# Bias rows in free partitions, a third stack buffer, a residual turned back by TensorE, and products that nobody reads

## The reference, cut to what matters

```python
for l in range(DEPTH):                                      # DEPTH = 2, ALPHA = sqrt(2)
    sh1, sc1, g1, sh2, sc2, g2 = split(silu(c) @ w_ada[l] + b_ada[l])     # c is one vector
    h = x * (1 + sc1) + sh1
    y = conformer_conv(h, ...) if l == 0 else fox_attention(...) @ w_o
    x = layer_norm(ALPHA * x + (1 + g1) * y, ln_mix_g[l], ln_mix_b[l])
    h = x * (1 + sc2) + sh2
    y = grouped_moe(h, router_w, router_b, w_gate[l], w_up[l], w_down[l])
    x = layer_norm(ALPHA * x + (1 + g2) * y, ln_ffn_g[l], ln_ffn_b[l])
# conformer_conv: u = a * sigmoid(b) of h @ w_pw1; y = 31-tap causal convolution per channel + b_dw;
#                 silu(layer_norm(y)) @ w_pw2 + b_pw2
# shared_kv (layer 1): silu(c) @ w_ada_kv + b_ada_kv shifts and scales x; k, v, forget gates from it
# grouped_moe: every token goes to two experts of one group, (silu(h @ w_gate) * (h @ w_up)) @ w_down
```

## Time and profile before

| | us |
|---|---|
| median of 3 runs | 1353.41 |
| lowest, highest | 1352.75, 1355.64 |
| the profiled execution, its time | 1354.2 |
| its span | 1352.2 |
| PE, DVE, ACT, POOL busy | 1087.2, 447.4, 168.2, 24.9 |
| HBM read | 492.19 MB, 365 GB/s over the span |

### The profile page before, as it was taken

One profiled execution on the slowest core, in us unless ns is written; L12 is line 12 of the kernel. 1 busy time (PEld: TensorE's weight loads), 2 busy tenths in 40 slices (PEclk: granted clock), 3 DMA queues, 4 the chain that ended last, 5 costly groups with the idle time before them and its releaser, 6 DMA issues.

```text
span 1352.2 us, 30588 instructions
## 1 busy us (share of the span) xinstructions
PE 1087.2 (80%) x12942; PEld 637.4 (47%) x12942; DVE 447.4 (33%) x1389; ACT 168.2 (12%) x401; POOL 24.9 (2%) x58
## 2 busy tenths in 40 slices
PE   3898978667999669766899979696699996796665
PEld 1784434334555235422475864353356663453333
DVE  0498145211333113211454340651133231231114
ACT  1103121000111001000210431210010110000001
POOL 1103000000000000000000000000000000000000
PEclk7899969978999689978999999698899998998888
DMA  9975579999999999999997531889999899999990
GB/s 360 385 288 194 234 314 427 425 425 426 425 424 424 426 426 425 424 425 423 418 418 310 248 125 64 371 363 423 425 427 425 340 411 425 425 425 423 425 412 35
DMA packets 56957, 494.70 MB, mean 366 GB/s; under 512 B 4196, under 2 KB 12420, under 8 KB 17176
## 3 DMA queue, kind: packets, MB, share of 16 engines
q1 hardware_dynamic: 55920, 490.75, 87.5%
q10 hardware_dynamic: 744, 2.35, 0.5%
q0 software_dynamic: 192, 0.15, 0.1%
HBM read 492.19 MB, written 1.05 MB: 365 GB/s over the span
## 4 chain that ended last, share of the span: by engine, by line
PE 52%; DMA 36%; DVE 7%; ACT 2%; issue 1%; POOL 1%; ACTq 1%; SPq 0%; DVEq 0%; POOLq 0%
PE PS L1041 22%; DMA ring<-in_w_up_dram 21%; DMA ring<-in_w_gate_dram 8%; PE PS L948 6%; PE PS L1155 4%; DMA ring<-in_w_down_dram 3%; PE PS L1069 3%; DMA work<-in_w_gate_dram 2%; PE PS L1020 2%; PE PS L1279 2%; PE PS L966 2%; PE PS L853 2%; DVE xs L1410 1%; DMA work<-in_conv_ln_b_dram 1%; PE PS L1032 1%
## 5 line engine op out<-in xcount | busy, mean ns | idle before, releaser
L1041 PE MATMUL PS<-ring,work 128*32 128x256 f32 x8160 | 522.5, 412 | 165.7 <-DMA ring<-in_w_up_dram 67.3
L1041 PEld LDWEIGHTS PS<-ring,work 128*32 128x32 f32 x8160 | 282.3, 117 | 391.5 <-issue 116.7
L1593 DVE TENSOR_TENSOR work<-work,PS 128x256 f32<-128x256 f32 x47 | 19.8, 422 | 435.8 <-PE PS L1041 434.5
L948 PE MATMUL PS<-ring,work 128*128 128x512 f32 x192 | 83.3, 594 | 0.5 <-ACT work L804 0.5
L674 ACT ACTIVATE work<-PS 128x256 f32<-128x256 f32 x47 | 18.1, 384 | 436.1 <-PE PS L1041 436.1
L1041 PE MATMUL PS<-work 128*32 128x256 f32 x864 | 56.4, 404 | 15.1 <-DMA work<-in_w_gate_dram 9.7
L1679 DVE SCALAR_TENSOR_TENSOR work<-work,colv 128x256 f32<-128x256 f32 x150 | 67.0, 503 | 1.2
L1020 PE MATMUL PS<-hs,work 128*32 128x256 f32 x784 | 55.6, 402 | 8.8 <-DVE work L1561 7.8
L1155 PE MATMUL PS<-work,ring 128*128 128x256 f32 x256 | 58.3, 392 | 2.5 <-ACT work L615 2.5
L1069 PE MATMUL PS<-work 32*128 32x256 f32 x784 | 56.1, 400 | 3.8 <-DVE work L1606 3.8
L853 PE MATMUL PS<-ring,cact 128*32 128x512 f32 x384 | 49.3, 664 | 11.2 <-DMA ring<-in_w_ada_dram 11.2
(11 more groups left out here) (239 smaller groups left out, 845.5 us busy)
## 6 DMA issues: line engine op xcount, KB each, us to landing
ring<-in_w_gate_dram SPq DMA_DIRECT2D x58, 2048.0 KB, 34.9
ring<-in_w_up_dram SPq DMA_DIRECT2D x58, 2048.0 KB, 34.8
ring<-in_w_down_dram SPq DMA_DIRECT2D x58, 2048.0 KB, 28.6
ring<-in_w_ada_dram SPq DMA_DIRECT2D x24, 2048.0 KB, 20.4
work<-in_w_up_dram SPq DMA_DIRECT2D x6, 2048.0 KB, 19.7
work<-in_w_gate_dram SPq DMA_DIRECT2D x6, 2048.0 KB, 34.7
work<-in_w_down_dram SPq DMA_DIRECT2D x6, 2048.0 KB, 42.7
ring<-in_w_pw_dram SPq DMA_DIRECT2D x8, 1024.0 KB, 12.1
```

The lines of the kernel that those rows point to most:

```text
L948: last = pe.matmul(PS[:, banks + 2 * t + q, :], rows[:, k, t * P:(t + 1) * P], quarter(index + h, kk, KH)[:, q * BANK:(q + 1) * BANK], sta ...
L1041: last = pe.matmul(dst[SLOTS * s:SLOTS * (s + 1), :], rows[:, cc, SLOTS * q:SLOTS * (q + 1)], quarter(load + h, kk, KH)[:, QUART * s:QUART ...
```

## The change

- **Rows.** `rows` gets rows 8 to 43 for the biases and 72 to 87 for the norms, as they lie in memory, by 7 transfers instead of 20, and a row 96 of ones. The ones and biases are no longer added by DVE (`plus` is gone): `bias_rows` does four matmuls (8 records) at the third load of each adaLN group, with a column of `ident` or of `row_or_one`, which picks the bias row alone or with the row of ones. In front of its first matmul it waits for the DVE addition of the group before.
- **Start.** The turning of `colrows` moves from ahead of load 1 to ahead of load 3. `columns` takes one group there, and the norms' columns (`lncol`, `rescol` with ALPHA) are turned after channel part 3.
- **Third stack** in `colrows`, without the wait for the first.
- **b_pw2** is put into the banks first, between mean and variance.
- **Norm.** ACT takes `copy_cols` and `keep_g2` behind its root and its half; ACT normalises 512 columns of token tile 1, DVE the other 512 and tile 0.
- **Residual.** `keep_x` behind the mixing norm and L689 are gone. ACT makes ALPHA*x, turned, from banks 0 to 3 in eight steps of 128x256 into `rT` (the memory of `xs`), and 32 matmuls (64 partitions, 64 columns each, by halves of the array) turn it back into banks 0 to 3.
- **`unread(n)`**: n matmuls 128x256 of constants, whose result is not read: 8 ahead of turning `hs` in both layers, 6 behind the residual of layer 1, 8 ahead of `sum_x` in both.
- The KV columns' addition moves behind `take_xT`; three of the KV loads come ahead of `sel_ready`.

```diff
 def ada_load(index, j, bank):
+    if j == 2:
+        bias_rows(index, bank)
     arrived(index + j)
...
+def bias_rows(index, bank):
+    pe.wait_ge(rows_in, ROWS)
+    pe.wait_ge(ada_added, adas[0])
...
+    for q in range(4):
...
+        last = pe.matmul(PS[32 * q:32 * q + 32, bank, :], from_row, rows[:, :], start=(index == L_ADA1_G0),
+                         stop=False, tile_position=(0, 32 * q), skip_group_check=True)
...
+def unread(products):
+    for _ in range(products):
+        pe.matmul(PS[:, B_Y, 0:SEQ], ident[:, :], cmask2[:, :, :].rearrange("p b n -> p (b n)"), start=True,
+                  stop=True, skip_group_check=True)
...
 # TensorE, moe(l), behind the logits
-                spread_ln(0, l, 0)
-                spread_ln(1, l, 2)
+                def residual():
+                    pe.wait_ge(rT_ready, l + 1)
+                    for t in range(TT):
+                        for k in range(KD):
+                            for half in range(2):
...
+                                pe.matmul(PS[:, bank, at:at + QUART - 3:KH], rT[of, k, t * P:(t + 1) * P], ident[of, of],
+                                          start=(t == 0 and k % KH == 0), stop=True, tile_position=(64 * half, 0),
+                                          skip_group_check=True)
                 if l == 0:
-                    for j in range(ADA_G // 2):
+                    for j in range(ADA_G - 1):
                         ada_load(L_ADAKV, j, B_GATE)
+                else:
+                    residual()
+                    unread(6)
                 pe.wait_ge(sel_ready, l + 1)
...
                 if l == 0:
-                    for j in range(ADA_G // 2, ADA_G):
-                        ada_load(L_ADAKV, j, B_GATE)
-                if l == 0:
-                    pe.wait_ge(ada_added, 4)
+                    ada_load(L_ADAKV, ADA_G - 1, B_GATE)
+                    residual()
+                unread(8)
...
 # ScalarE, moe(l), behind the exponential
+                for k in range(KD):
+                    last = act.activation(rT[:, k, :], PS[:, k // 2, (k % 2) * SEQ:(k % 2 + 1) * SEQ], ACT.Identity,
+                                          bias=rescol[:, 2 + l, k:k + 1], scale=rescol[:, l, k:k + 1])
+                last.then_inc(rT_ready, 1)
...
-                act.wait_ge(spread_used, (3, 8)[l])
-                for b in range(4):
-                    act.activation(PS[:, b, :].rearrange("p (t n) -> p t n", t=TT), xs[:, :, b * QUART:(b + 1) * QUART],
-                                   ACT.Copy, scale=ALPHA).then_inc(sums_begun, 1)
...
 # TensorE, layer 0: from the projection to the turn
-            project(L_PW2, 0, chunk_ready=z_ready)
...
+            project(L_PW2, 0, y_ready, chunk_ready=z_ready, begun=True)
             pe.wait_ge(ada_added, 2)
             spread_mod(0, 2, 4)
             ada(L_ADA0_G2, 6)
             pe.wait_ge(ada_added, 3)
             spread_g2(0)
-            columns(7, 1, 3)
+            columns(7, 2, 4)
+            unread(8)
             turn_n(1)
             moe(L_MOE0, 0)
```

More of the change, by code:

```diff
@@ L581, in _, with load_rows @@
         def _(act):
[L582 to L584 removed]
+            def load_rows(row, src):
+                act.dma_start(rows[row:row + src.shape[0], :], src).then_inc(rows_in, 16)
             for t in range(TT):
@@ L876, in spread_row @@
                 for i in range(2):
-                    q, r = row(i)
-                    last = pe.matmul(PS[:, bank + i, :], pick(q, r, P), rows[32 * q:32 * q + 32, :], start=True, stop=True,
-                                     tile_position=(32 * q, 0), skip_group_check=True)
+                    strip = slice(row(i) // 32 * 32, row(i) // 32 * 32 + 32)
+                    last = pe.matmul(PS[:, bank + i, :], ident[strip, row(i):row(i) + 1].to_broadcast([32, P]), rows[strip, :],
+                                     start=True, stop=True, tile_position=(strip.start, 0), skip_group_check=True)
                     if i == 0:
@@ L934, in h_there, with project @@
                 pe.wait_ge(hT_copied, 4 * hs_turned[0])
-            def project(index, banks, done=None, chunk_ready=None, rows=hT, between=None):
+            def project(index, banks, done, chunk_ready=None, moving=hT, between=None, begun=False):
                 for h in range(2):
@@ L1127, in _ @@
             turn_h(lambda t, k: by_chunk(xs[:, t, :])[:, k // KH, k % KH, :])
[L1128 to L1133 removed]
+            for j in range(1, ADA_G):
+                if j == ADA_G - 1:
+                    pe.wait_ge(colrows_in, COLROWS)
+                    for k in range(KD):
+                        last = pe.transpose(PS[:, 6, k * 40:k * 40 + NROWS], colrows[0:NROWS, k * P:(k + 1) * P],
+                                            ident[0:NROWS, 0:NROWS])
+                    last.then_inc(cols_turned, 1)
                 ada_load(L_ADA0_G0, j, 4)
             pe.wait_ge(ada_added, 1)
[L1136 removed]
+            columns(5, 1, 2)
             h_there()
@@ L1147, in _ @@
                     last.then_inc(taps_spread, 1)
+                if f == 3:
+                    for j in range(4):
+                        last = pe.matmul(PS[:, 5, 16 * j:16 * (j + 1)], rows[:, j:BANK:4], ident[:, NORM_ROW:NORM_ROW + 16],
+                                         start=True, stop=True, skip_group_check=True)
+                        if j == 0:
+                            behind(last)
+                    last.then_inc(lncol_done, 1)
                 if f >= 4:
@@ L1207, in _ @@
             last.then_inc(mean_done, 1)
+            pe.wait_ge(brow_in, 16 * 4)
+            for t in range(TT):
+                for q in range(2):
+                    r = 32 * (2 * t + q)
+                    pe.matmul(PS[:, 2 * t + q, :], ones[r:r + 1, :], brow[r:r + 1, q * BANK:(q + 1) * BANK],
+                              start=True, stop=False, skip_group_check=True)
             for k in range(KD):
@@ L1214, in _ @@
                 ada_load(L_ADA0_G1, j, 4)
-            pe.wait_ge(brow_in, 16 * 4)
-            project(L_PW2, 0, chunk_ready=z_ready)
-            for t in range(TT):
-                for q in range(2):
-                    r = 32 * (2 * t + q)
-                    last = pe.matmul(PS[:, 2 * t + q, :], ones[r:r + 1, :], brow[r:r + 1, q * BANK:(q + 1) * BANK],
-                                     start=False, stop=True)
-            last.then_inc(y_ready, 1)
+            project(L_PW2, 0, y_ready, chunk_ready=z_ready, begun=True)
             pe.wait_ge(ada_added, 2)
@@ L1359, in _ @@
             pe.wait_ge(ada_added, 7)
-            columns(7, 4, 6)
+            columns(7, 5, 7)
+            unread(8)
             turn_n(3)
```

180 lines of the change are left out of this document (92 added, 88 removed).

## The result

| | median, us | ratio to the kernel before |
|---|---|---|
| before | 1353.76 (16 runs) | |
| changed | 1360.17 (16 runs, 1354.91 to 1368.85) | 1.0046 (1.0034 to 1.0059) |

The forecast was 8.1 us faster; the kernel is about 6 us slower. A fence shows the first profile where nothing else is said.

A forecast was written before the change was run, and what follows sets the result against it. Bound: the stream of loads plus its halts when no ring slot is free. Sum: -6.0 - 1.6 + 0.9 - 8.2 + 0.9 + 5.9 = -8.1 us, 1353.4 to 1345.3; range 1339.5 to 1351.5.

The forecast's parts named there:

- Start: Up to the convolution: colrows sooner, loads 1 and 2 done ahead, load 3 ends at 30.5 for 36.4; gain 6.0 us.
- The 3.8 us for thirteen transfers: At the start: thirteen transfers of 0.29 us of issue each go, so colrows come 3.8 us sooner, near 24.
- Convolution's end: Before the mean: without the third stack's 7.86 us, TensorE comes early and waits for VectorE; gain 1.6 us.
- the worst case of POOL's products: In the convolution: POOL's four products beside VectorE's earlier taps may cost 1.4 us at worst; 0 was taken.
- bias_rows: In each adaLN group: eight records of 0.11 us cost 0.9 us, counted where they lie on the path.
- Pause of layer 0: Behind layer 0's projection: first KV load at 22.0 us, slot freed sooner, 8.2 of 8.5 us of standing gained.
- the lid: Layer 0's pause: five loads keep the stream busy until 26.6 us behind the projection, so releases by 25.1 gain the same.
- the cover: Layer 0's pause: three freed loads last to 41.6, gathering at 38.5, so work ahead is free; up to 3 us otherwise.
- Between the layers: From layer 0's experts to the second projection's end: +0.9 us, for bias_rows between two halves of the V projection.
- Pause of layer 1: Behind layer 1's projection: residual (5.8 us) and six products (2.8) precede the count; release at 45.4 for 39.5, loss 5.9.
- rival C: Layer 1's pause: the residual's halves don't overlap, 9.3 us and not 5.8; -4.6 in all, 1348.8 us; chance 0.21.
- Rival D: Both pauses: unread products don't keep the clock, only take time; layer 1 loses 22.9, total +16.4, 1369.8 us; chance 0.09.

The follow-up runs named there:

- e8: The changed kernel with 13 small transfers of 8 numbers each put back ahead of colrows on ScalarE's queue: 1361.99 us, 1.0056 of the kernel before.
- e2: The changed kernel without any unread products, the function and its four calls removed: 1350.50 us, 0.9982 of the kernel before.
- e3: The changed kernel with the norms' rows in four groups of 32 partitions, two read by the spreads here: 1355.44 us, 1.0009 of the kernel before.
- again: The changed kernel measured and profiled once more with no edit: 1359.69 us, 1.0047 of the kernel before.
- e6: Changed kernel, norm rows in four groups, residual behind first expert's gate/up products, unread products only in layer 1 (ten behind logits, seven behind count): 1342.43 us, 0.9909.

## Why the prediction was wrong

**Start: right in kind, -5.5 for -6.0 at best, and -4.6 in the mean.** Load 3 came at 29.3 and not 27, and its sixteen records took 1.92 us, not the 3.5 that I took. The two errors cancel in the first profile (and 36.4 less my 30.5 is 5.9, not 6.0). In the others load 3 took up to 3.64 us, and L1209 starts between 36.7 and 38.6. The 3.8 us for thirteen transfers were not what paid (e8).

**Convolution's end: the step failed.** I said that TensorE would come to the mean early and wait for VectorE. It is TensorE's own queue that comes last: VectorE ends at 120.0, the mean at 121.4. And the change puts the norms' columns, which were in the group of 48 columns ahead of L1155, as eight records of their own between the projections at 60.75, 1.7 us on that queue; I left them out. The 1.4 us that I called the worst case of POOL's products is what VectorE pays at its earlier taps (10.72 for 9.29), and 0.9 of it comes back at the last ones; I had taken 0. It doesn't show, because VectorE is not what comes last. Gain 0.7 for 1.6.

**bias_rows: right.** 1.04 us a group where it is on the path, 0.9 taken.

**Pause of layer 0: the lid was right, the cover wrong.** A gain with nothing behind it is there: 7.3 us in e2, 4.7 to 5.6 in four more profiles, for the 8.2 that I took. In the changed kernel it is 4.1 in the first profile and 2.2 in the mean. Three terms: the eight products ahead of the turn took 5.39 us instead of 3.6, since the clock fell to 0.50 while they ran; the KV loads behind them ran at half clock (6.31 for two); and so the gathering stood at 43.3, behind the 41.6 that I had worked out as its limit and from which I had called all that stands ahead of it free. "It costs up to 3 us if that cover is gone" is what happened. A further 1 us was overlooked. Before, the projection's last product itself frees its slot. In the changed kernel that product signals `y_ready`, the slot is freed with the first product of the spread behind it, and SP's first issue behind the projection (its end at 163.61 before, 158.24 after) moved from 0.04 to 1.09 us behind it. SP's queue, before and after:

```profile
163.65 4.13 SPq L447 DMA_DIRECT2D ring<-in_w_gate_dram  x2
```

```profile
159.33 2.22 SPq L452 DMA_DIRECT2D ring<-in_w_gate_dram  x2
```

With it the first profile closes: 8.3 less 3.2 us of standing less 1.05 is about 4, for 4.1. The 2 us by which the mean gains less lie in the experts behind the pause, or in the chance of before's one profile; no trace here says which.

**Between the layers: a term was missing.** +4.9 for +0.9. `bias_rows` in `sum_acc` is the 0.9. The sum has no term for the two spreads of the norm between the halves of the K projection: I didn't ask on which partitions their rows now lie. Before, the four products read four different groups of 32 rows and ran side by side in 1.14 us; now all read one group and take 3.69, one after the other. The Trainium skill (TensorE: Matmul & The Clock Gate, The mechanism) says that a weight load overlaps with running matmuls only where its row group is another, and that in this way small products on different row groups overlap; the trace agrees, with 1.14, 1.99 and 3.69 us on four, two and one. So 2.5 us are the spreads, and the clock behind them is 1.3 in the mean (e3); with the 0.9 that is 4.7 of the 4.9.

**Pause of layer 1: the mechanism was right, and the clock's part was mis-sized.** The residual's halves overlap, against rival C: 64 records in 3.79 us at full clock. But the clock was down for all of it, 7.09 for 5.8, and for most of the six products, 4.96 for 2.8. The count came at 37.7 for 35.4, the release at 47.8 for 45.4, a loss of 8.4 in the pause for 5.9. The 5.8 rested on a misread row. I had the clock back at 197.2 "4 to 5 us into work" and began that work at 193.07. But TensorE was at work from 189.26 without a pause, as the ten busy microseconds from 190 to 200 in the earlier trace rows say:

```profile
189.26 1.86 PE L993 MATMUL PS<-lane,work 128*128 128x16 f32 x8 [0.70 <-DVE work L1495]
191.05 2.09 PE L878 MATMUL PS<-rows,ident 32*128 32x512 f32 x8
```

The return came 7.9 us behind the start of that work. Priced by that, the residual runs at half clock throughout, 7.0 us by the prediction's own figures. Rival D (the products don't keep the clock) had the right reason; it put the size at 22.9 because it took everything at half clock.

**The rivals.** The range ended at 1351.5 because every unknown was bounded in one pause alone. Outside of D, no rival had the gain of layer 0 fall to a third together with a loss of 8 in layer 1, though both hang on the same clock.

## What to carry to other kernels

Work that fills a pause must be put behind everything that somebody waits for, not only into the pause: ask for each product which ready instruction it stands ahead of, on its own engine's queue, and what its price is at the low clock. The same residual cost 8 us ahead of the count and nothing that shows behind the release, and unread products cost 4 us (sixteen) and 9 us (all 38) where ready work stood behind them, and nothing where TensorE stood. When rows are moved to other partitions, look up which products that ran side by side now read the same rows.

## What the runs showed of the hardware

The granted clock can fall under a TensorE that is never idle: while the two spreads ran one after the other on one group of 32 rows, the clock fell (in `again` from 1.00 to 0.50 between 691.0 and 691.5, some 3.5 us into them), and the products behind them lost 1.5 to 2.9 us in five of eight profiles, and none in the five in which the two spreads read two groups. A product that nobody reads doesn't hold the clock by itself either: behind the columns of layer 0 it was at 0.50 from 171 to 174 while eight of them ran (5.39 us for 3.70). In the pause of layer 1 ten of them began at half clock at 853.67 in e6, and it was at 1.00 from 857, before they ended. Four products of POOL beside VectorE's taps cost VectorE 1.4 us at one place (10.72 for 9.30) and 0.9 at another (18.56 for 17.62). And two executions of one kernel can differ by 11 us in their spans with both pauses the same to 0.5 us.
